# Decoder layer with product-key experts: 26 instead of 22 key sums computed as dense blocks, gate sums used straight from PSUM, table places and chunk spacing changed

## The chip, the cores and the metric

The kernel runs on one core of one Trainium2 chip. The metric is device time in microseconds of one launch; lower is better. TensorE (PE) multiplies matrices into PSUM, VectorE (DVE), ScalarE (ACT) and GpSimd (POOL) do the rest, SyncE (SP) and GpSimd's queue start the DMA transfers, and 16 DMA engines carry them all.

## What is computed

One decoder layer for 256 tokens of width 1024: two kinds of self attention, a cross attention, and then the part that the change is about, a product-key expert layer:

```python
def peer(h, w_q, sub_keys, u, v):
    q = (hf @ w_q).reshape(T, PEER_HEADS, 2, PEER_KEY_DIM // 2)
    sc = jnp.einsum('thpc,pkc->thpk', q, sub_keys).astype(jnp.float32)
    v1, i1 = lax.top_k(sc, PEER_TOPK)                       # 16 of 128 keys, twice
    ...                                                     # 16 best of the 256 pairs
    gates = jax.nn.softmax(top, axis=-1)
    def token_block(args):
        xc, ec, gc = args
        a = jax.nn.gelu(jnp.einsum('cd,ced->ce', xc, u[ec]), approximate=False)
        return jnp.einsum('ce,ced->cd', gc * a, v[ec])
```

Each of 256 tokens picks 8 x 16 = 128 of 16384 experts. An expert has a row of `u` and a row of `v`, 1024 floats each. A final rmsnorm follows.

## The kernel before

**Gathered slots.** The 32768 (token, expert) pairs are worked off in 256 slots. A slot is one expert for each of 128 tokens: GpSimd starts an indirect DMA that fetches up to 128 rows of 8 KB (`u` and `v` side by side) into a buffer of a ring; DVE multiplies the `u` half with the token's row and sums (`dot`, L2266); ACT applies gelu, the gate, and writes the weight on a diagonal matrix (`weigh`, L1608, L1614, L1622); PE multiplies diagonal by `v` half and sums in PSUM (`use_pair`, L1211 and L1214). PE, ACT and the buffers go by groups of two slots: group i holds slots 2i and 2i+1. Slots 0 to 127 belong to the first 128 tokens, 128 to 255 to the others.

**Blocks.** Expert rows are sorted on the host by key sum, (first key - second key) mod 128. The first 106 key sums (`GATHERED_KEYS`) are gathered. The other 22 (`BLOCKS`) are blocks of 128 experts that are computed densely for all 256 tokens; rows of theirs in a slot are left out of the gather by its bounds check. A block needs a 512 KB table of `u`, an *up product* (8 matmuls of 128x256, `up_product`, L1261), gelu into `in_block_acts` (`take_up`, ACT), a multiplication with the token's gate, and a *down product* with a 512 KB table of `v` (4 matmuls of 128x512 for both halves of the tokens, `weigh_block`, L1294).

**Tables.** SP loads the 44 tables in order (L801) into `tables`, four places: two over `x`, two over buffers given up by the ring. Table j waits until table j-4 has been used.

**Gate sums.** How much gate a token gives to each expert of the blocks is found in 16 chunks of 16 tokens. For a chunk DVE builds a one-hot matrix (`onehot`, L2315) and, for every second chunk, a list of gates (`listed_gates`, L2330 and L2335); PE multiplies them (`token_gates`, 32 small matmuls, L1282) into a PSUM bank; ACT copies the bank to `gate_sums` (`take_gates`, L1693); DVE multiplies it onto the activations (`weigh_acts`, L2342). Before a chunk's `weigh_acts` DVE waits for that copy.

**The order** is written out by hand in tables that are keyed by slot (DVE) or by group (PE, ACT). Up products stand behind groups 36 to 58; chunk q starts at slot 118 + 4q, its `token_gates` stands behind group (start + 2) // 2, its `weigh_acts` at slot start + 7; down products stand behind groups 94 to 116, two (block, half) pairs in most. Each engine's queue is in order. The ring has 12 to 14 buffers at first; five are given up for activations, one-hots and tables between slots 67 and 104, which leaves 10; one joins at slot 134 and one at slot 194 (`JOINS`). Gather n is issued only when PE has used the slot that had its buffer.

Of the kernel before, what the change touches and what calls it, by code (L numbers as in the profile page):

```python
# [17 lines left out]
D = 1024  # L18
S = 256
# [51 lines left out]
QUERIES_FIRST = 3  # L71


BLOCKS = 22
GATHERED_KEYS = PEER_KEYS - BLOCKS
GATHERED = GATHERED_KEYS * PEER_KEYS
EXPERTS = PEER_KEYS * PEER_KEYS
# [43 lines left out]

TURN_BEHIND = {7: 0, 9: 1}
TAKE_TURN_BEHIND = {8: 0, 10: 1}
UP_FROM, UP_TO = 36, 60
UP_PARTS = 1
UP_BEHIND, TAKE_UP_BEHIND = {}, {}
for n in range(UP_PARTS * BLOCKS):
# [6 lines left out]
COUNT_AT = 90  # L134
ONEHOT_AT = {}
GATHER_GATES_BEHIND = {}
TAKE_GATES_BEHIND = {}
WEIGHTS_AT = {}
for q in range(TOKEN_CHUNKS):
    begun = 118 + 4 * q  # L140
    ONEHOT_AT[begun] = q
    GATHER_GATES_BEHIND[(begun + 2) // GROUP] = q
    TAKE_GATES_BEHIND[(begun + 2) // GROUP + 1] = q
    WEIGHTS_AT[begun + 7] = q
DOWN_FROM, DOWN_TO = 94, 117
# [24 lines left out]
RAW_LOADED = [name for name in PANELS if name not in LOADED_EARLY]  # L170
FIRST_BUFFERS = [0, 5, 8, 2, 3, 4, 9, 10, 11, 12]
PRODUCT_BUFFER = 13
JOINS = {22: 14, 24: 15, 58: 6, 67: 7, 79: 1, 134: 16, 194: 11}
JOINED_BEHIND = {134: f"up{BLOCKS // 2 - 1}", 194: f"token_gates{TOKEN_CHUNKS - 1}"}
GIVEN_FROM = {15: 67, 14: 70, 10: 86, 11: 102, 12: 104}
BACK = {JOINS[n]: n for n in JOINED_BEHIND}

# [62 lines left out]
def product_order():  # L240


    order = []

    def add(name, engine):
        order.append((name, engine))

    for c in range(4):
        add(f"turn_mix{c}", "both")
    for j in range(15):  # L250
        add(f"qkv{j}", "act")
        if j == 0:
            add("line", "dve")
            add("keys", "act")
    for r in range(SOFTMAXES):
        for s in self_slots(r):
            add(f"score{s}", "dve")
        if r in GATE_AFTER_SCORES:
            add(f"gate{GATE_AFTER_SCORES[r]}", "act")
    for r in range(SOFTMAXES + 1):  # L260
        if r < SOFTMAXES:
            for s in self_slots(r):
                add(f"probs_t{s}", ("act", "dve")[s % 2])
        if r in GATE_AFTER_TURN:
            add(f"gate{GATE_AFTER_TURN[r]}", "act")
        if r >= 1:
            add(f"self_o{r - 1}", "both")
    for c in range(4):
        add(f"turn_mem{c}", "both")
    for branch in "AB":  # L270
        for c in range(4):
            add(f"branch{branch}{c}", "dve")
    add("kv0", "act")
    add("kv1", "act")
    for j in range(4):
        add(f"out{j}", "dve")
    add("kv2", "act")
    for c in range(4):
        add(f"turn_cross{c}", "both")
    add("kv3", "act")  # L280
    for j in range(2):
        add(f"qcross{j}", "act")
    for h in range(CROSS_HEADS):
        add(f"cross_score{h}_0", "act")
    for i in range(2):
        add(f"cross_probs_t{i}_0", "act")
    for i in range(2):
        add(f"cross_o{i}_0", "both")

    def cross_output(t):  # L290
        for j in range(2):
            add(f"ocross{j}_{t}", "dve")

    def turned_rows(t):
        for half in range(2):
            add(f"turn{t}_{half}", "both")

    def query(h, t):
        add(f"qpeer{h}_{t}", "act")
# [12 lines left out]
    add("cross_o0_1", "act")
    add("cross_o1_1", "act")
    cross_output(1)
    query(1, 0)
    turned_rows(1)
    for kind in ("qpeer", "qturn", "key_score"):
        for h in range(2):
            add(f"{kind}{h}_1", "act")
    query(2, 0)  # L320
    query(2, 1)

    for i in range(GROUPS):
# [12 lines left out]
        if i in GATHER_GATES_BEHIND:
            add(f"token_gates{GATHER_GATES_BEHIND[i]}", "act")
    return order


# [33 lines left out]
def build(nc, x_in, mem_in, rel_bias, panels, keys_in, experts, up_in, gain_cols, gain_rows, ident_in,  # L374
          onehot_in, mask_in, iota_in, count_in, out):
    with ExitStack() as ctx:
# [145 lines left out]
        def slot(n):  # L522
# [17 lines left out]
        in_block_acts = given[:, 0:BLOCKS * S].rearrange("p (b t) -> p b t", b=BLOCKS)  # L540
        onehots = [given[:, at:at + PEER_KEYS * CHUNK // 2].bitcast(F16).rearrange("p (e t) -> p e t", e=PEER_KEYS)
                   for at in (8 * D, 9 * D)]
        gate_sums = given[:, BLOCKS * S:BLOCKS * S + SUMS * CHUNK * BLOCKS].rearrange("p (s b t) -> p s b t", s=SUMS, b=BLOCKS)
        tables = [x[:, 0, :], x[:, 1, :]] + [given[:, at:at + D] for at in (6 * D, 7 * D)]
        last_squares, gained = given[:, 5 * D:6 * D], given[:, 6 * D:6 * D + 512]

        by_lists = scores.rearrange("p (u c) -> p u c", u=UNITS)
# [134 lines left out]
        count_step = sem("count_step")  # L682
        onehot_step = sem("onehot_step")
        onehot_ready = sem("onehot_ready")
        blocks_gated = sem("blocks_gated")
        blocks_weighed = sem("blocks_weighed")
        crossed_out = sem("crossed_out")
        crossed_summed = sem("crossed_summed")
# [120 lines left out]
        def _(pe):  # L809
# [477 lines left out]
            def weigh_block(block, t):  # L1287

                if block == 0:
                    pe.wait_ge(blocks_gated, TOKEN_CHUNKS)  # L1290
                down = table(BLOCKS + block)
                for half in range(2):
                    cols = slice(half * 512, (half + 1) * 512)
# [72 lines left out]
        def _(act):  # L1366
# [316 lines left out]
                    took(nc.scalar.copy(rowsT[:, 4 * half:4 * half + 4, t * P:(t + 1) * P],  # L1683
                                        b.rearrange("p (k c) -> p k c", k=4)))

            def take_gates(q):

                b = take(f"token_gates{q}")
                if q == 0:
                    act.wait_ge(slot_free, LAST_IN[12] + 1)  # L1690
                if q >= SUMS:
                    act.wait_ge(blocks_gated, q - SUMS + 1)
                took(nc.scalar.activation(gate_sums[:, q % SUMS], b[:, 0:CHUNK * BLOCKS].rearrange(  # L1693
                    "p (b t) -> p b t", b=BLOCKS), ACT.Copy, scale=1.0 / GATE_SCALE))
# [21 lines left out]
            def take_up(j):  # L1716

                b = take(f"up{j}")
                if j % 4 == 0:
                    act.wait_ge(slot_free, LAST_IN[(14, 10, 12)[j // 4]] + 1)  # L1720
                took(nc.scalar.activation(in_block_acts[:, 2 * j:2 * j + 2, :].rearrange("p a b -> p (a b)"), b,
                                          ACT.Gelu))

# [9 lines left out]
            for i in range((UNITS - 1) * TOPK // GROUP):  # L1733
# [27 lines left out]
                    take_row_turn(TAKE_TURN_BEHIND[i])  # L1761
                if i in TAKE_UP_BEHIND:
                    take_up(TAKE_UP_BEHIND[i])
                if i in TAKE_GATES_BEHIND:
                    take_gates(TAKE_GATES_BEHIND[i])
                if i == PEER_HEADS * TOPK // GROUP:
                    for half in range(2):
                        take_crossed(0, half, PEER_HEADS * TOPK)
# [34 lines left out]
        def _(dve):  # L1803
# [533 lines left out]

            def weigh_acts(q):

                dve.wait_ge(taken["act"], taken_count(f"token_gates{q}"))  # L2340
                part_of_acts = in_block_acts[:, :, q * CHUNK:(q + 1) * CHUNK]
                nc.vector.tensor_tensor(part_of_acts, part_of_acts, gate_sums[:, q % SUMS], ALU.mult  # L2342
                                        ).then_inc(blocks_gated, 1)

            def last_weight_diag(s):

# [276 lines left out]
```

## Time and profile before

| | us |
|---|---|
| median of 3 runs (lowest, highest) | 916.57 (915.57, 924.42) |
| the profiled execution, its own time | 915.18 |
| its span, first to last instruction | 913.1 |
| PE, DVE, ACT, POOL busy in it | 821.2, 643.6, 419.8, 388.4 |

The span is 2.1 us shorter than the execution's own time. Attention and the first queries take the first 300 us; the gathers run from about 295 to 900. PE is busy 90% of the span, but in some stages it waits and in others it never does, so the rows below are read by stage. A busy DMA share of 1.00 means all 16 engines were busy all the time.

### The profile page before, as it was taken

The page shows a single profiled execution, that of the slowest core. Times are in us where ns is not written, and L with a number is a line of the kernel's source. Part 1 is how long each engine was busy: PE and PEld are TensorE (multiplying, and loading weights), DVE is VectorE, ACT ScalarE, POOL GpSimd, SP SyncE. Part 2 cuts the span into 40 slices and gives each one's busy share as a digit, 9 for nine tenths or more (in the row PEclk, how much of TensorE's full clock was granted, in tenths as well). Part 3 has the DMA queues.
Part 4 walks back from the last instruction along what each step waited for, and adds up shares of the span by engine and source line. Part 5 has one row for each costly group of instructions (what it writes and reads, how often), then busy time and mean ns, then how long its engine had stood idle before and what let it go on. Part 6 is the DMA issues. An engine that isn't in the chain of part 4 may idle for free.

```text
span 913.1 us, 15434 instructions
## 1 busy us (share of the span) xinstructions
PE 821.2 (90%) x5656; PEld 528.7 (58%) x5656; DVE 643.6 (70%) x1467; ACT 419.8 (46%) x1075; POOL 388.4 (43%) x307
## 2 busy tenths in 40 slices
PE   9999999999999778697699999989778869999975
PEld 8999998799987634354256666634334423333311
DVE  5444686465657897979998999968888754444565
ACT  6534556345556566445455446433344332222243
POOL 1000055122002577466664444557757744434470
PEclk9999999999999999898999999979999889999988
DMA  8898434156353999999999999999999999999993
GB/s 303 236 228 231 169 119 159 55 215 251 127 207 125 367 377 420 417 406 417 417 416 416 415 410 412 412 416 416 419 416 415 419 418 408 415 416 415 412 397 148
DMA packets 55602, 302.62 MB, mean 331 GB/s; under 512 B 11904, under 2 KB 15348, under 8 KB 22674
## 3 DMA queue, kind: packets, MB, share of 16 engines
q0 software_dynamic: 37152, 222.64, 59.7%
q1 hardware_dynamic: 15544, 76.13, 22.9%
q10 hardware_dynamic: 2832, 2.88, 2.3%
q8 instruction: 44, 0.72, 0.3%
q14 instruction: 30, 0.25, 0.1%
HBM read 345.90 MB, written 1.54 MB: 381 GB/s over the span
## 4 chain that ended last, share of the span: by engine, by line
PE 63%; DMA 14%; DVE 9%; ACT 6%; issue 6%; POOL 2%; POOLq 0%; SPq 0%; DVEq 0%; ACTq 0%
PE y L1211 15%; PE ps L1261 9%; DMA arena<-in_experts,arena 8%; PE y L1294 8%; PE ps L825 6%; PE ps L826 6%; PE ps L827 6%; DVE late_ring L2266 3%; PE ps L868 2%; DMA rowsT<-in_experts,arena 2%; DVE w_lo L1818 2%; DMA late_ring<-in_experts,arena 2%; DMA late_ring<-in_experts,expert 2%; ACT w_hi L1388 1%; ACT diag L1622 1%
## 5 line engine op out<-in xcount | busy, mean ns | idle before, releaser
L2474 POOL DMA_INDIRECT arena<-in_experts,arena x148 | 197.8, 1337 | 154.2 <-PE ps L1214 116.4
L2266 DVE CUSTOM_DVE_ANT_0 late_ring<-arena 128x1024 f32<-128x1024 f32 x158 | 192.2, 1222 | 83.4 <-DMA arena<-in_experts,arena 75.1
L1211 PE MATMUL y<-arena,diag 64*64 64x512 f32 x600 | 154.5, 637 | 43.1 <-ACT diag L1622 39.6
L1214 PE MATMUL ps<-arena,diag 64*64 64x512 f32 x616 | 157.8, 633 | 0.0
L1608 ACT ACTIVATE acts<-dots 128x2 f32<-128x2 f32 x125 | 25.3, 202 | 256.9 <-DVE dots L2266 234.9
L1818 DVE TENSOR_TENSOR w_lo<-raw,w_hi 128x2048 fp32r<-128x2048 f32 x36 | 84.9, 2360 | 70.2 <-ACT w_hi L1388 70.2
L2266 DVE CUSTOM_DVE_ANT_0 late_ring<-late_ring,arena 128x1024 f32<-128x1024 f32 x82 | 99.7, 1220 | 30.5 <-DMA late_ring<-in_experts,arena 23.3
L2474 POOL DMA_INDIRECT late_ring<-in_experts,arena x63 | 80.4, 1276 | 73.8 <-PE ps L1214 61.6
L1211 PEld LDWEIGHTS y<-arena,diag 64*64 64x64 f32 x600 | 37.5, 137 | 127.9 <-issue 69.7
L1211 PE MATMUL y<-late_ring,diag 64*64 64x512 f32 x328 | 82.5, 624 | 21.6 <-ACT diag L1622 19.8
L1388 ACT CAST w_hi<-raw 128x2048 fp32r<-128x2048 f32 x37 | 70.4, 1904 | 50.2 <-DMA raw<-in_panels 36.9
L1622 ACT ACTIVATE diag<-ident,acts 128x128 f32<-128x128 f32 x250 | 86.8, 394 | 4.8 <-PE ps L1214 0.8
L825 PE MATMUL ps<-h_hi,w_hi 128*128 128x256 f32 x304 | 86.9, 286 | 0.0
L826 PE MATMUL ps<-h_lo,w_hi 128*128 128x256 f32 x304 | 86.0, 283 | 0.0
L827 PE MATMUL ps<-h_hi,w_lo 128*128 128x256 f32 x304 | 86.0, 283 | 0.0
L2446 POOL TENSOR_SCALAR arena<-arena,row_inv 128x128 f32<-128x128 f32 (+3 forms) x24 | 25.7, 1084 | 119.6 <-DVE row_inv L1887 119.4
L1214 PE MATMUL ps<-late_ring,diag 64*64 64x512 f32 x280 | 70.0, 619 | 0.0
L825 PEld LDWEIGHTS ps<-h_hi,w_hi 128*128 128x128 f32 x304 | 58.3, 192 | 2.3 <-issue 2.0
L826 PEld LDWEIGHTS ps<-h_lo,w_hi 128*128 128x128 f32 x304 | 58.3, 192 | 0.0
L827 PEld LDWEIGHTS ps<-h_hi,w_lo 128*128 128x128 f32 x304 | 58.3, 192 | 0.0
L1211 PEld LDWEIGHTS y<-late_ring,diag 64*64 64x64 f32 x328 | 20.2, 136 | 64.4 <-issue 35.9
L1614 ACT ACTIVATE acts<-acts,arena 128x1 f32<-128x1 f32 x218 | 52.3, 287 | 4.4
(359 smaller groups left out, 1796.3 us busy)
## 6 DMA issues: line engine op xcount, KB each, us to landing
raw<-in_panels SPq DMA_DIRECT2D x40, 1024.0 KB, 4.9
arena<-in_panels SPq DMA_DIRECT2D x6, 1024.0 KB, 7.1
x<-in_up SPq DMA_DIRECT2D x12, 512.0 KB
late_ring<-in_experts SPq DMA_DIRECT2D x12, 512.0 KB
late_ring<-in_up SPq DMA_DIRECT2D x10, 512.0 KB
x<-in_experts SPq DMA_DIRECT2D x10, 512.0 KB
arena<-line_scratch ACTq DMA_DIRECT2D x8, 320.0 KB, 7.8
arena<-in_experts,arena POOLq DMA_INDIRECT x148
```

What stands on the lines that cost most here:

```text
L825: pe.matmul(dst, stationary[0], moving[0], start=first, stop=False)
L826: pe.matmul(dst, stationary[0], moving[1], start=False, stop=False)
L827: return pe.matmul(dst, stationary[1], moving[0], start=False, stop=last)
L1211: straight = pe.matmul(y[rows, t, cols], diag[rows, a % DIAGS, rows], slot(a)[rows, down], start=False, stop=False, skip_group_check=True)
L1214: across = pe.matmul(ps[to, half, :], diag[rows, b % DIAGS, rows], slot(b)[rows, down], start=first, stop=False, skip_group_check=True)
L1261: mm = pe.matmul(b[:, block % 2 * S:(block % 2 + 1) * S], up[:, k * P:(k + 1) * P], rowsT[:, k, :], start=(k == 0), stop=(k == CHUNKS - 1))
L1294: mm = pe.matmul(y[:, t, cols], in_block_acts[:, block, t * P:(t + 1) * P], down[:, cols], start=False, stop=False, skip_group_check=True)
L1388: nc.scalar.copy(split_parts(n)[0], raw_panel(n)).then_inc(w_hi_ready, 1)
L1622: i = nc.scalar.activation(diag[:, s % DIAGS, :], ident[:], ACT.Copy, scale=acts[:, s:s + 1])
L1818: nc.vector.tensor_tensor(low, raw_panel(n), high.bitcast(F32), ALU.subtract).then_inc(w_lo_ready, 1)
L2266: i = nc.vector.tensor_tensor_reduce(row if n < len(FIRST_BUFFERS) else products[s % GROUP], row, h_rows[:, u // PEER_HEADS, :], 1.0, 0.0, ...
L2474: nc.gpsimd.indirect_dma_start(out=slot(n), out_offset=None, in_=experts, in_offset=bass.IndirectOffsetOnAxis(ap=expert_rows(u)[:, s:s + 1 ...
```

## The change

- `BLOCKS` goes from 22 to 26, so 102 key sums are gathered. Four more up products, down products and pairs of tables; all chunk operands over blocks grow from 22 to 26 columns.
- The tables have three places instead of four: the activations now reach into the buffer that held two of them.
- `take_gates` on ACT and `gate_sums` are gone. `weigh_acts` reads the PSUM bank itself, scales and multiplies in one DVE operation, and waits for `token_gates` on PE.
- Up products stand behind groups 34 to 59. Chunks start every three slots, at 118 + 3q, and `weigh_acts` stands six slots after the start instead of seven. Down products stand behind groups 86 to 116, one or two pairs each. The ring gets its buffer back at slot 180 instead of 194.

```diff
-BLOCKS = 22
+BLOCKS = 26
...
-UP_FROM, UP_TO = 36, 60
+UP_FROM, UP_TO = 34, 61
...
 for q in range(TOKEN_CHUNKS):
-    begun = 118 + 4 * q
+    begun = 118 + 3 * q
     ONEHOT_AT[begun] = q
     GATHER_GATES_BEHIND[(begun + 2) // GROUP] = q
-    TAKE_GATES_BEHIND[(begun + 2) // GROUP + 1] = q
-    WEIGHTS_AT[begun + 7] = q
-DOWN_FROM, DOWN_TO = 94, 117
+    WEIGHTS_AT[begun + 6] = q
+DOWN_FROM, DOWN_TO = 86, 117
...
-JOINS = {22: 14, 24: 15, 58: 6, 67: 7, 79: 1, 134: 16, 194: 11}
+JOINS = {22: 14, 24: 15, 58: 6, 67: 7, 79: 1, 134: 16, 180: 11}
...
-            add(f"token_gates{GATHER_GATES_BEHIND[i]}", "act")
+            add(f"token_gates{GATHER_GATES_BEHIND[i]}", "dve")
...
-        tables = [x[:, 0, :], x[:, 1, :]] + [given[:, at:at + D] for at in (6 * D, 7 * D)]
+        tables = [x[:, 0, :], x[:, 1, :]] + [given[:, at:at + D] for at in (BLOCKS * S,)]
...
-            def take_gates(q):
-
-                b = take(f"token_gates{q}")
-                if q == 0:
-                    act.wait_ge(slot_free, LAST_IN[12] + 1)
-                if q >= SUMS:
-                    act.wait_ge(blocks_gated, q - SUMS + 1)
-                took(nc.scalar.activation(gate_sums[:, q % SUMS], b[:, 0:CHUNK * BLOCKS].rearrange(
-                    "p (b t) -> p b t", b=BLOCKS), ACT.Copy, scale=1.0 / GATE_SCALE))
...
             def weigh_acts(q):
 
-                dve.wait_ge(taken["act"], taken_count(f"token_gates{q}"))
+                if q == 0:
+                    dve.wait_ge(taken["act"], taken_count(f"up{BLOCKS // 2 - 1}"))
+                b = take(f"token_gates{q}")
                 part_of_acts = in_block_acts[:, :, q * CHUNK:(q + 1) * CHUNK]
-                nc.vector.tensor_tensor(part_of_acts, part_of_acts, gate_sums[:, q % SUMS], ALU.mult
-                                        ).then_inc(blocks_gated, 1)
+                took(nc.vector.scalar_tensor_tensor(part_of_acts, b[:, 0:CHUNK * BLOCKS].rearrange(
+                    "p (b t) -> p b t", b=BLOCKS), 1.0 / GATE_SCALE, part_of_acts, ALU.mult, ALU.mult))
```

PE around the start of the up products, before. L868 is the last query product, L1211 and L1214 use a group of slots (four rows a group), L1180 is a key score, L1261 an up product:

```order
2144 L868 MATMUL ps<-rowsT,arena 128x256 x8
2145 L1211 MATMUL y<-late_ring,diag 64x512 x2
2146 L1214 MATMUL ps<-late_ring,diag 64x512 x2
2147 L1211 MATMUL y<-late_ring,diag 64x512 x2
2148 L1214 MATMUL ps<-late_ring,diag 64x512 x2
2149 L1211 MATMUL y<-arena,diag 64x512 x2
2150 L1214 MATMUL ps<-arena,diag 64x512 x2
2151 L1211 MATMUL y<-arena,diag 64x512 x2
2152 L1214 MATMUL ps<-arena,diag 64x512 x2
2153 L1180 MATMUL ps<-keysT,qpT 128x128 x4
```

The same place after; its lines are five lower, so L1256 is the up product:

```order
2144 L863 MATMUL ps<-rowsT,arena 128x256 x8
2145 L1206 MATMUL y<-late_ring,diag 64x512 x2
2146 L1209 MATMUL ps<-late_ring,diag 64x512 x2
2147 L1206 MATMUL y<-late_ring,diag 64x512 x2
2148 L1209 MATMUL ps<-late_ring,diag 64x512 x2
2149 L1256 MATMUL ps<-rowsT,x 128x256 x8
2150 L1206 MATMUL y<-arena,diag 64x512 x2
2151 L1209 MATMUL ps<-arena,diag 64x512 x2
2152 L1206 MATMUL y<-arena,diag 64x512 x2
2153 L1209 MATMUL ps<-arena,diag 64x512 x2
2154 L1175 MATMUL ps<-keysT,qpT 128x128 x4
2155 L1256 MATMUL ps<-rowsT,x 128x256 x8
```

Groups 34 and 35 have up products behind them now, where they stood back to back. The second place is DVE in the middle of the chunks, before (L2266 is a dot, whose second row reads out its sum):

```order
1004 L2342 TENSOR_TENSOR late_ring<-late_ring 128x22x16
1005 L2266 ISA late_ring,dots<-arena 128x1024
1006 L2266 ISA dots 128x1
1007 L2315 TENSOR_TENSOR late_ring<-counts,column_of 128x2048
1008 L2266 ISA late_ring,dots<-late_ring,arena 128x1024
1009 L2266 ISA dots 128x1
1010 L2266 ISA late_ring,dots<-arena 128x1024
1011 L2266 ISA dots 128x1
1012 L2266 ISA late_ring,dots<-arena 128x1024
1013 L2266 ISA dots 128x1
1014 L2342 TENSOR_TENSOR late_ring<-late_ring 128x22x16
```

And after, where L2249 is a dot, L2327 `weigh_acts`, L2298 `onehot`, L2313 and L2318 `listed_gates`:

```order
1014 L2327 SCALAR_TENSOR_TENSOR late_ring<-ps,late_ring 128x26x16
1015 L2298 TENSOR_TENSOR late_ring<-counts,column_of 128x2048
1016 L2249 ISA late_ring,dots<-arena 128x1024
1017 L2249 ISA dots 128x1
1018 L2249 ISA late_ring,dots<-arena 128x1024
1019 L2249 ISA dots 128x1
1020 L2249 ISA late_ring,dots<-arena 128x1024
1021 L2249 ISA dots 128x1
1022 L2327 SCALAR_TENSOR_TENSOR late_ring<-ps,late_ring 128x26x16
1023 L2313 TENSOR_TENSOR raw<-raw,row_of 128x832
1024 L2318 TENSOR_TENSOR gates_even<-raw,gate_piece 128x1664
1025 L2298 TENSOR_TENSOR late_ring<-counts,column_of 128x2048
```

There were four dots between two `weigh_acts`; there are three. Between a chunk's `onehot` and its `weigh_acts` there are six dots instead of seven.

## Rows read from the trace of the kernel before

**Rows 1.** Busy time by stretch; columns PE, PEld, DVE, ACT, POOL, then PEclk, DMA share, GB/s.

```profile
300.00:340.00 40.00, 29.78 (x239) 18.77 (x237) 36.93 (x123) 23.47 (x67) 24.17 (x18) 1.00 0.95 374
346.00:473.00 127.00, 102.17 (x668) 52.08 (x657) 112.76 (x355) 66.89 (x209) 75.70 (x59) 0.93 1.02 416
473.00:597.00 124.00, 124.00 (x730) 77.26 (x722) 113.53 (x361) 62.61 (x192) 60.59 (x45) 1.00 1.02 413
597.00:706.00 109.00, 87.58 (x838) 44.30 (x834) 90.15 (x145) 42.16 (x146) 73.77 (x53) 0.92 1.02 417
706.00:745.00 39.00, 28.12 (x241) 11.60 (x241) 26.38 (x43) 13.23 (x48) 24.50 (x20) 0.85 1.02 418
745.00:867.00 122.00, 122.00 (x532) 43.23 (x528) 57.00 (x93) 31.77 (x116) 53.53 (x45) 0.99 1.01 414
867.00:896.00 29.00, 19.65 (x129) 5.18 (x132) 17.54 (x31) 13.29 (x39) 18.49 (x14) 0.84 0.99 398
```

**Rows 2.** DMA by queue: q0 the gathers, q1 SP's transfers; packets, MB, share.

```profile
q0 software_dynamic: 37152, 222.64, 59.7%
q1 hardware_dynamic: 15544, 76.13, 22.9%
```

**Rows 3.** The chain of work, up products: start us, us, what.

```profile
469.70 1.85 issue
...
473.51 3.65 PE ps L1261 x16
...
479.04 3.65 PE ps L1261 x16
...
597.21 0.65 PE y L1211 x2
```

**Rows 4.** The chain of work, down products.

```profile
751.53 3.63 PE y L1294 x8
...
757.04 3.63 PE y L1294 x8
```

**Rows 5.** DVE's groups from 600 to 745: busy us, mean ns, idle before.

```profile
L2266 DVE CUSTOM_DVE_ANT_0 late_ring<-arena 128x1024 f32<-128x1024 f32 x50 | 60.8, 1225 | 20.8 <-DMA arena<-in_experts,arena 16.6 <-issue 3.9
L2315 DVE TENSOR_TENSOR late_ring<-counts,column_of 128x2048 f16<-128x2048 f16 x14 | 17.1, 1219 | 0.0
...
L2342 DVE TENSOR_TENSOR late_ring<-late_ring 128x352 f32<-128x352 f32 x16 | 8.3, 521 | 1.3 <-ACT late_ring L1693 1.3
...
L2330 DVE TENSOR_TENSOR raw<-raw,row_of 128x704 f16<-128x704 f16 x7 | 3.6, 520 | 0.0
L2335 DVE TENSOR_TENSOR raw<-raw,gate_piece 128x1408 f16<-128x1408 f16 x4 | 3.6, 893 | 0.1
```

**Rows 6.** A DVE operation of the new kind, from PSUM, 128x512.

```profile
L2386 DVE SCALAR_TENSOR_TENSOR x<-y,rstd,raw 128x512 f32<-128x512 f32 x2 | 1.4, 746 | 0.0
```

**Rows 7.** Timeline inside a chunk: start us, us, engine, what, idle before.

```profile
644.96 1.22 DVE L2266 CUSTOM_DVE_ANT_0 late_ring<-arena 128x1024 f32<-128x1024 f32 x1
...
646.11 1.23 DVE L2266 CUSTOM_DVE_ANT_0 late_ring<-rowsT,arena 128x1024 f32<-128x1024 f32 x1
...
648.93 0.65 PE L1211 MATMUL y<-arena,diag 64*64 64x512 f32 x2 [0.41 <-ACT diag L1622]
...
650.81 2.22 PE L1282 MATMUL ps<-raw,late_ring 128*128 128x22 f16 x32
```

**Rows 8.** The chain of work: gathers from issue to landing, and a group at the lower clock.

```profile
642.57 14.02 DMA late_ring<-in_experts,arena
...
715.27 1.12 PE y L1211 x2
716.40 0.84 PE y L1211 x2
```

**Rows 9.** SP's timeline: a table is issued.

```profile
477.19 0.33 SPq L801 DMA_DIRECT2D x<-in_up  x1
```

**Rows 10.** DMA by queue, 480.2 to 484.4, behind that issue.

```profile
q1 hardware_dynamic: 143, 0.52, 31.1%
```

More of the change, by code:

```diff
@@ L82 @@
 PIECES = 2
-SUMS = 1
 TO_WHOLE = 1.5 * 2 ** 23
@@ L136 @@
 GATHER_GATES_BEHIND = {}
-TAKE_GATES_BEHIND = {}
 WEIGHTS_AT = {}
 for q in range(TOKEN_CHUNKS):
-    begun = 118 + 4 * q
+    begun = 118 + 3 * q
     ONEHOT_AT[begun] = q
     GATHER_GATES_BEHIND[(begun + 2) // GROUP] = q
-    TAKE_GATES_BEHIND[(begun + 2) // GROUP + 1] = q
-    WEIGHTS_AT[begun + 7] = q
-DOWN_FROM, DOWN_TO = 94, 117
+    WEIGHTS_AT[begun + 6] = q
+DOWN_FROM, DOWN_TO = 86, 117
 DOWN_BEHIND = {}
@@ L172 @@
 PRODUCT_BUFFER = 13
-JOINS = {22: 14, 24: 15, 58: 6, 67: 7, 79: 1, 134: 16, 194: 11}
-JOINED_BEHIND = {134: f"up{BLOCKS // 2 - 1}", 194: f"token_gates{TOKEN_CHUNKS - 1}"}
+JOINS = {22: 14, 24: 15, 58: 6, 67: 7, 79: 1, 134: 16, 180: 11}
+JOINED_BEHIND = {134: f"up{BLOCKS // 2 - 1}", 180: f"token_gates{TOKEN_CHUNKS - 1}"}
 GIVEN_FROM = {15: 67, 14: 70, 10: 86, 11: 102, 12: 104}
@@ L542, in build @@
                    for at in (8 * D, 9 * D)]
-        gate_sums = given[:, BLOCKS * S:BLOCKS * S + SUMS * CHUNK * BLOCKS].rearrange("p (s b t) -> p s b t", s=SUMS, b=BLOCKS)
-        tables = [x[:, 0, :], x[:, 1, :]] + [given[:, at:at + D] for at in (6 * D, 7 * D)]
+        tables = [x[:, 0, :], x[:, 1, :]] + [given[:, at:at + D] for at in (BLOCKS * S,)]
         last_squares, gained = given[:, 5 * D:6 * D], given[:, 6 * D:6 * D + 512]
@@ L684, in build @@
         onehot_ready = sem("onehot_ready")
-        blocks_gated = sem("blocks_gated")
         blocks_weighed = sem("blocks_weighed")
@@ L1289, in weigh_block @@
                 if block == 0:
-                    pe.wait_ge(blocks_gated, TOKEN_CHUNKS)
+                    pe.wait_ge(taken["dve"], taken_count(f"token_gates{TOKEN_CHUNKS - 1}"))
                 down = table(BLOCKS + block)
@@ L1719, in take_up @@
                 if j % 4 == 0:
-                    act.wait_ge(slot_free, LAST_IN[(14, 10, 12)[j // 4]] + 1)
+                    act.wait_ge(slot_free, LAST_IN[(14, 10, 12, 15)[j // 4]] + 1)
                 took(nc.scalar.activation(in_block_acts[:, 2 * j:2 * j + 2, :].rearrange("p a b -> p (a b)"), b,
@@ L1763, in _ @@
                     take_up(TAKE_UP_BEHIND[i])
-                if i in TAKE_GATES_BEHIND:
-                    take_gates(TAKE_GATES_BEHIND[i])
                 if i == PEER_HEADS * TOPK // GROUP:
```

## The prediction

> **What bounds the kernel now.** I read the windows by stage first, since PE's 821.2 of 913.1 us is an average over stages with different limits. From 346 to 867 the DMA engines are busy all the time at 413 to 418 GB/s [rows 1]: the reader is to see that this column hardly moves while PE's does. PE is busy throughout in two stages, 473 to 597 (up products) and 745 to 867 (down products), and waits in the others. So both are near their limits. What separates them is the chain of waits: in the two product stages it runs along PE, one block and one group of slots each 5.53 us (up: 473.51 to 479.04) and 5.51 us (down: 751.53 to 757.04) [rows 3, 4]; elsewhere it steps over to gathers of 14.0 us from issue to landing [rows 8]. A gather carries 222.64 / 256 = 0.870 MB [rows 2], which is 2.09 us at 417 GB/s; 14.0 us are then 6.7 gathers in flight. Behind 867 PE has little left and the end hangs on the last 17 slots landing.
>
> **Bytes.** Gathers fall by 4 of 106 key sums: 222.64 x 4/106 = 8.40 MB less; 8 more tables of 0.524 MB are 4.19 MB more. Net 4.21 MB, at 415 GB/s 10.1 us. Some 20 slots run before the engines are full (374 GB/s at share 0.95 [rows 1]), where PE, DVE and the issuing set the pace; I give them no saving: 20 x 0.033 MB = 0.66 MB, 1.6 us. If the DMA engines stayed as full as they are, the end would come 8.5 us earlier.
>
> **Up products.** Four more cost 4 x 3.65 = 14.6 us of PE [rows 3], in a stage where PE has no gap. Two things give back. The groups before it come some 4.5 us earlier through fewer bytes (about 70 slots x 0.033 MB, less the first 20, and one table less ahead: 1.65 + 0.52 MB would be 5.2 us; I take 4.5), and between groups 35 and 36 PE stood still for 1.85 us [rows 3], about 2 with its surroundings. So group 60, which starts at 597.2 [rows 3], starts at 597.2 + 14.6 - 4.5 - 2 = 605.3. The transfers need less than that: a group now asks for 2 x 0.837 + 0.524 = 2.20 MB in 5.53 us, 397 GB/s, where 413 were moved [rows 1]. PE binds alone here, and over 26 blocks the engines lose 26 x 5.53 x (1 - 397/413) = 5.6 us. Part is only borrowed: the number in flight can fall first. How low it may fall before engines idle the trace doesn't show; from 6.7 down to about 5 is 1.7 slots, 3.4 us, and I take 3 us lost (between 0 and 5.6).
>
> **Chunks.** DVE's work for six slots (two chunks, one list) now: six dots at 1.15 us (back to back, start to start [rows 7]) 6.9; two one-hots 2 x 1.22 = 2.44; list 0.52 x 832/704 + 0.89 x 1664/1408 = 1.67; two `weigh_acts`. The new operation has no row of its own: the old one is 0.52 us for 352 columns, one of the same kind from PSUM 0.75 for 512 [rows 5, 6]; I take 0.62 for 416, nearer to the second in kind (0.58 to 0.75). Sum 12.25 us, 2.04 a slot, against 0.837/0.417 = 2.01 for the transfer. Before, eight slots with the same two chunks were 9.2 + 2.44 + 1.41 + 1.04 = 14.1 us, 1.76 a slot against 2.09, which is why DVE waits for gathers there [rows 5]. **The cover is gone.** The 16 ACT copies that are removed lay on an engine that was busy 42 of 109 us [rows 1], and DVE waited 1.3 us for them in all [rows 5]: nothing by themselves. The wait of `weigh_acts` moves to PE. From the end of the second dot of a group PE starts it after 1.67 us (646.11 + 1.15 = 647.26 to 648.93), the group takes 1.88 (to 650.81) and the 32 gate products 2.2 [rows 7]: 5.8 us. For an even chunk DVE fills this with `weigh_acts`, one-hot and three dots, 0.62 + 1.22 + 3.45 = 5.3, so it waits 0.5 to 0.65; for an odd one the list lies between as well and there is no wait. Behind that wait stand DVE's dots, and behind these ACT and PE. So 12.9 us for six slots, 2.15 a slot. Groups 60 to 86 (52 slots) become about 111 us, where they were 706 - 597 = 109. Group 86 starts at 605.3 + 111 = 716. The transfers of this stage, 52 x 0.837 + about 0.8 MB of tables, would take 106 us: 4 to 5 us more lost.
>
> **Down products.** They start behind group 86: 31 groups x 1.88 + 52 x 1.815 = 152.7 us on PE, if nothing waits, against 31 x 2 x 0.837 + 23 x 0.524 = 64 MB, 154 us, for the transfers. These balance; the last down product ends at about 869, where it ended at 867 [rows 1]. PE gets the 10 us back that it was late, because it now has work in 706 to 745, where it was busy 28 of 39 us.
>
> **The end.** By bytes: 913.1 - 8.5 + 3 + 4 = 911.6. By the chain: 869 instead of 867, but with some two slots more landed by then (2 x 1.93), so 913.1 + 2 - 3.9 = 911.2. I take a span of 911.2; with the 2.1 us around it 913.3, 1.9 below the profiled execution's 915.2. The median of the runs was 1.4 above that execution, so 914.7.
>
> **One rule weighed.** The trace has gathers only in a crowd, so it shows 14.0 us and not how few would do [rows 8]. The Trainium skill, "DMA: Bandwidth & Descriptors", section "Bandwidth", gives 6.15 us of engine time for a single 1 MB transfer. By that three or so in flight would keep the engines full, the up products would lose nothing, and the end would be another 3 us earlier, an estimate from that page. The row at 374 GB/s and share 0.95 speaks against taking it whole. The sum doesn't use it.
>
> **Rivals.**
> 1. *The transfers stay full.* The queue in flight absorbs both late stages and bytes alone decide: 8.5 us less, 908 span, about 908 to 909 as median. For: the share is 1.02 in every stage, even with 10 buffers. Against: 397 GB/s asked for by a stage in which PE has no gap is arithmetic, not a guess.
> 2. *Slower: the wait of `weigh_acts` on PE.* The even chunks' handshake has nothing to spare. A group at the lower TensorE clock takes 1.12 + 3 x 0.84 = 3.64 us instead of 1.88 [rows 8], and the granted clock averaged 0.92 in this stage, after PE had waited for diagonals. If most even chunks meet that, DVE waits 2.3 instead of 0.6 us, eight times: 13 us later at group 86. The rest of the program cannot make it good, as the down stage is full on both sides. With 0 to 5 us more from fewer gathers in flight: 924 to 931. It decides from about 0.5 us of delay per chunk. The Trainium skill, "TensorE: Matmul & The Clock Gate", section "HAM oscillation", tells of a kernel whose clock falls at every wait for DMA; by that each such group would be slow here too. The trace shows it for some groups, and PE will have fewer gaps than before.
> 3. *Three table places stall PE.* A table issued at 477.19 has all its 0.52 MB moved by 484.4, 7.2 us [rows 9, 10]. With three places it has two periods and a group, 2 x 5.53 + 1.87 = 12.9 us. Only if a table took as long as a gather (14.0) would PE wait, 1.1 us at each of some 48 tables, 50 us at most; I count 930 to 945.
>
> **How the numbers follow.** Forecast (908 to 921 around 914.7) 0.68; rival 1 (904 to 909) 0.12; rival 2 (922 to 931) 0.16; rival 3 0.04. One per cent, 9.2 us, is about what a measurement of this kernel can tell from no change. Faster by over that (below 907.4) takes most of rival 1 and a little of the forecast's edge: 0.12. Slower by over that (above 925.7) takes two thirds of rival 2 and rival 3: 0.15. The range leaves out the lower half of rival 1, the upper part of rival 2 and rival 3: 907 to 926.
>
> **What the profile after would show.** Gathers 214 MB, SP's queue 80 MB. PE without a gap from about 461 to 605, with 5.53 us between up products; GB/s in that stage about 400 instead of 413. Six slots in the chunks take 12.9 us, DVE is busy over 90% of it, and a new row has `weigh_acts` of 0.62 us waiting for L1277, 4 to 8 us in all. Down products end near 869. Rival 1 shows 413 or more in all stages; rival 2 shows waits over 12 us on L1277 and group 86 behind 722; rival 3 shows up products that wait for a table. I am wrong if DVE reaches the chunks so far ahead that it never binds, or if the engines idle already with five in flight.

## The result and the profile after

The kernel after takes 927.35 us (median of 4, 925.6 to 929.44) beside 916.07 before (4, 915.08 to 924.42): ratio 1.0116, interval 1.0089 to 1.0142, 11 us slower. The profiled execution took 929.44 us, 2.1 over the median. Its head and the page's rows on its queues and on two kinds of DMA (count, KB where given, median us from issue to landing):

```profile
span 927.6 us, 15608 instructions
...
q0 software_dynamic: 37152, 214.20, 58.0%
q1 hardware_dynamic: 16696, 80.32, 23.6%
...
arena<-in_experts,arena POOLq DMA_INDIRECT x146, 12.1
...
x<-in_up SPq DMA_DIRECT2D x18, 512.0 KB, 8.2
```

The bytes fell as the change says: 4.25 MB less than in [rows 2]. The same view by stage as [rows 1] (PE, PEld, DVE, ACT, POOL, PEclk, DMA share, GB/s), of after; its stages are: before the up products, up products, chunks, down products, the end:

```profile
346.00:468.00 122.00, 103.01 (x656) 51.25 (x656) 109.42 (x345) 69.46 (x212) 77.46 (x57) 0.92 1.01 413
468.00:611.00 143.00, 142.75 (x826) 90.91 (x826) 122.30 (x384) 64.96 (x203) 67.53 (x50) 1.00 0.98 380
611.00:722.00 111.00, 97.60 (x944) 52.71 (x946) 94.06 (x150) 37.29 (x133) 72.14 (x50) 0.91 0.98 381
723.00:881.00 158.00, 152.31 (x692) 52.27 (x692) 76.21 (x125) 42.70 (x155) 81.99 (x65) 1.00 1.02 416
881.00:910.60 29.60, 18.19 (x133) 4.45 (x132) 18.38 (x33) 14.08 (x42) 16.55 (x13) 0.94 1.00 411
```

Read the last column. Before, it stood at 413 to 418 up to 867. Now 254 us of the middle run at 380, first with PE busy without a gap, then with DVE waiting for PE. The engines' share shows almost nothing of it, 0.98 instead of 1.02. At 413 and 417 GB/s the same bytes would have taken 143 x (1 - 380/413) = 11.4 us and 111 x (1 - 381/417) = 9.6 us less.

The chain of work of after, where it turns from up products to chunks, inside the chunks, and in the down stage (start us, us, what):

```profile
468.25 3.72 PE ps L1256 x16
...
602.11 3.65 PE ps L1256 x16
607.64 3.65 PE ps L1256 x16
613.16 2.17 PE ps L1277 x32
...
676.12 0.83 PE y L1206 x2
676.98 0.83 PE y L1206 x2
679.80 2.17 PE ps L1277 x32
684.05 1.22 DVE late_ring L2298
```

The up products are on the chain one behind another, still 5.53 us apart as in [rows 3], 26 of them now. Behind them the chain goes PE (gate sums), DVE, PE, DVE. DVE's row for the new operation, 611 to 722 (busy us, mean ns, idle before), and then some of it in the timeline, with what DVE waited for:

```profile
L2327 DVE SCALAR_TENSOR_TENSOR late_ring<-ps,late_ring 128x416 f32<-128x416 f32 x16 | 9.4, 589 | 17.6 <-PE ps L1277 17.6
```

```profile
615.43 0.59 DVE L2327 SCALAR_TENSOR_TENSOR late_ring<-ps,late_ring 128x416 f32<-128x416 f32 x1 [7.58 <-PE ps L1277]
...
642.45 0.59 DVE L2327 SCALAR_TENSOR_TENSOR late_ring<-ps,late_ring 128x416 f32<-128x416 f32 x1 [0.63 <-PE ps L1277]
...
654.95 0.59 DVE L2327 SCALAR_TENSOR_TENSOR late_ring<-ps,late_ring 128x416 f32<-128x416 f32 x1 [0.63 <-PE ps L1277]
...
668.48 0.59 DVE L2327 SCALAR_TENSOR_TENSOR late_ring<-ps,late_ring 128x416 f32<-128x416 f32 x1 [1.74 <-PE ps L1277]
...
681.99 0.59 DVE L2327 SCALAR_TENSOR_TENSOR late_ring<-ps,late_ring 128x416 f32<-128x416 f32 x1 [1.72 <-PE ps L1277]
```

The first of the eight waits is PE's backlog: DVE is at chunk 0 at 607.9, PE still in its up products until 611.3. From there to 718 DVE waits for PE at these eight places and for no gather: it sets the pace of the chunks. Of the other seven (all at even chunks), two are 0.63 us and their six slots take 12.5 us; five are 1.7 to 1.8 us, and their six slots take 13.5. In front of the long ones PE's group runs at 0.83 us a pair of matmuls, as in the chain at 676.12, so at the lower of TensorE's two clocks (granted clock of the stage 0.91); just before it PE had stood 1.8 to 2.0 us for a diagonal, each time. In front of the two short ones PE had stood 0.3 to 0.5 us and its groups run at full speed.

The up stage in pieces, of after, and the piece of before that lies like the fourth:

```profile
478.00:500.00 22.00, 22.00 (x129) 13.79 (x128) 20.67 (x69) 9.75 (x31) 9.75 (x8) 1.00 1.00 400
500.00:520.00 20.00, 20.00 (x120) 12.03 (x119) 14.58 (x49) 9.85 (x31) 8.15 (x7) 1.00 0.97 357
520.00:540.00 20.00, 20.00 (x119) 13.01 (x121) 15.33 (x54) 12.67 (x37) 8.35 (x7) 1.00 1.01 406
540.00:558.00 18.00, 18.00 (x111) 10.76 (x102) 17.62 (x65) 5.79 (x23) 7.59 (x5) 1.00 0.87 307
558.00:611.00 53.00, 53.00 (x304) 34.01 (x303) 44.31 (x116) 24.43 (x74) 26.95 (x20) 1.00 1.00 394
```

```profile
540.00:558.00 18.00, 18.00 (x112) 10.76 (x108) 17.62 (x58) 8.77 (x27) 7.62 (x7) 1.00 1.01 409
```

So 380 is no steady rate. It is near 400 with two dips, to 357 and to 307.

### The profile page after: what moved, and what is told of

It is laid out like the page before. It is cut to its first block, busy times and chain, and to the rows that moved or that the text cites. A ratio compares the mean times of both kernels' runs of the same rounds, so it can differ in the third digit from the quotient of the medians.

```text
span 927.6 us, 15608 instructions
## 1 busy us (share of the span) xinstructions
PE 851.8 (92%) x5752; PEld 547.1 (59%) x5752; DVE 644.1 (69%) x1467; ACT 413.7 (45%) x1061; POOL 394.8 (43%) x307
## 4 chain that ended last, share of the span: by engine, by line
PE 62%; DMA 13%; DVE 12%; ACT 7%; issue 4%; POOL 1%; DVEq 0%; POOLq 0%; SPq 0%; ACTq 0%
PE y L1206 16%; DMA arena<-in_experts,arena 12%; PE ps L1256 10%; PE ps L820 6%; PE ps L822 6%; PE ps L821 6%; PE y L1289 5%; DVE late_ring L2249 4%; PE ps L1277 2%; ACT diag L1617 2%; PE ps L863 2%; DVE w_lo L1801 2%; ACT w_hi L1383 1%; PE ps L979 1%; DVE late_ring L2298 1%
## 5 line engine op out<-in xcount | busy, mean ns | idle before, releaser
L2459 POOL DMA_INDIRECT arena<-in_experts,arena x146 | 202.0, 1384 | 131.6 <-PE ps L1209 97.7
L2249 DVE CUSTOM_DVE_ANT_0 late_ring<-arena 128x1024 f32<-128x1024 f32 x158 | 191.1, 1221 | 69.7 <-DMA arena<-in_experts,arena 66.4
L1209 PE MATMUL ps<-arena,diag 64*64 64x512 f32 x736 | 191.7, 645 | 0.0
L1206 PE MATMUL y<-arena,diag 64*64 64x512 f32 x472 | 126.2, 661 | 23.6 <-ACT diag L1617 23.6
L1206 PE MATMUL y<-late_ring,diag 64*64 64x512 f32 x416 | 108.1, 642 | 21.1 <-ACT diag L1617 20.7
L2459 POOL DMA_INDIRECT late_ring<-in_experts,arena x65 | 83.5, 1285 | 89.2 <-PE ps L1209 72.4
L2249 DVE CUSTOM_DVE_ANT_0 late_ring<-late_ring,arena 128x1024 f32<-128x1024 f32 x82 | 99.5, 1218 | 27.1 <-DMA late_ring<-in_experts,arena 24.5
L1206 PEld LDWEIGHTS y<-arena,diag 64*64 64x64 f32 x472 | 30.9, 142 | 89.5 <-issue 50.4
L1206 PEld LDWEIGHTS y<-late_ring,diag 64*64 64x64 f32 x416 | 26.6, 140 | 81.1 <-issue 45.6
L1256 PE MATMUL ps<-rowsT,x 128*128 128x256 f32 x288 | 66.9, 385 | 1.3 <-ACT qpT L1641 1.3
L1256 PEld LDWEIGHTS ps<-rowsT,x 128*128 128x128 f32 x288 | 53.2, 190 | 21.7 <-issue 12.2
L1289 PE MATMUL y<-x,late_ring 128*128 128x512 f32 x136 | 64.4, 608 | 0.0
## 6 DMA issues: line engine op xcount, KB each, us to landing
arena<-in_experts,arena POOLq DMA_INDIRECT x146, 12.1
```

Of the source, the lines that this page charges most:

```text
L1206: straight = pe.matmul(y[rows, t, cols], diag[rows, a % DIAGS, rows], slot(a)[rows, down], start=False, stop=False, skip_group_check=True)
L1209: across = pe.matmul(ps[to, half, :], diag[rows, b % DIAGS, rows], slot(b)[rows, down], start=first, stop=False, skip_group_check=True)
L1256: mm = pe.matmul(b[:, block % 2 * S:(block % 2 + 1) * S], up[:, k * P:(k + 1) * P], rowsT[:, k, :], start=(k == 0), stop=(k == CHUNKS - 1))
L1289: mm = pe.matmul(y[:, t, cols], in_block_acts[:, block, t * P:(t + 1) * P], down[:, cols], start=False, stop=False, skip_group_check=True)
L2249: i = nc.vector.tensor_tensor_reduce(row if n < len(FIRST_BUFFERS) else products[s % GROUP], row, h_rows[:, u // PEER_HEADS, :], 1.0, 0.0, ...
L2459: nc.gpsimd.indirect_dma_start(out=slot(n), out_offset=None, in_=experts, in_offset=bass.IndirectOffsetOnAxis(ap=expert_rows(u)[:, s:s + 1 ...
```

## The experiments

Ratios are to the kernel before, timed on the same chip in the same job (median 915.2 to 916.2), with 95% intervals. Where a gain over the kernel after is given in us, it is the difference of two medians from different jobs; by the ratios it comes out up to 0.7 us smaller or larger. The first four were chosen to part the blocks, their PE time and their bytes from the rest.

**The blocks alone** (an edit of before; its chunks, down products and ACT copies are as they were):

```diff
-BLOCKS = 22
+BLOCKS = 26
-        tables = [x[:, 0, :], x[:, 1, :]] + [given[:, at:at + D] for at in (6 * D, 7 * D)]
+        tables = [x[:, 0, :], x[:, 1, :]] + [given[:, at:at + D] for at in (7 * D,)]
-                    act.wait_ge(slot_free, LAST_IN[(14, 10, 12)[j // 4]] + 1)
+                    act.wait_ge(slot_free, LAST_IN[(14, 10, 12, 15)[j // 4]] + 1)
```

> The kernel before with 26 blocks and nothing else of the change (three table places, because the activations cover the fourth; up products behind the old groups, chunks every four slots with the copy on ScalarE, down products behind groups 94 to 116). Theory A (four more products in a stage where PE has no gap slow it, and starve the transfers): up products end some 14 us later than before, the chunks go at the transfers' pace, down products end near 885, 926 to 932 us in all. Theory B (the three-slot chunks and DVE's wait on PE are what costs): chunks are as before here, so the time is at or below that of before, 908 to 917.

932.02 us, 1.0174 (1.0153 to 1.0196). The four blocks cost 16 us, more than the whole change. The windows of its up stage, of chunks and what follows up to the down products, and of the down products:

```profile
477.00:615.00 138.00, 138.00 (x793) 89.07 (x786) 116.89 (x365) 62.39 (x193) 61.36 (x47) 1.00 0.97 374
615.00:752.00 137.00, 111.92 (x1077) 55.69 (x1075) 113.59 (x182) 55.31 (x189) 97.36 (x70) 0.95 1.02 414
752.00:887.00 135.00, 135.00 (x564) 48.92 (x560) 61.15 (x100) 32.51 (x120) 58.48 (x48) 1.00 1.00 401
```

Most of the loss is in the up stage: 374 GB/s there, which is 138 x (1 - 374/413) = 13 us, and 414 behind it. A smaller part is in the down products, at 401 GB/s instead of 414: with the old start behind group 94 PE has no gap there either and sets the pace for 135 us, some 4 us of transfers. The rest of the change then gives 4.7 us of the 16 back. Its down stage, begun at group 86, runs at 416 GB/s.

**Everything but the blocks** (an edit of after):

```diff
-BLOCKS = 26
+BLOCKS = 22
-        tables = [x[:, 0, :], x[:, 1, :]] + [given[:, at:at + D] for at in (BLOCKS * S,)]
+        tables = [x[:, 0, :], x[:, 1, :]] + [given[:, at:at + D] for at in (6 * D,)]
```

> The changed kernel with 22 blocks again, all the rest of the change kept. Theory A: PE gets its 14.6 us back in the up products and as much in the down products, so it is near the kernel before, 912 to 919 us. Theory B: the chunk stage still has its waits of DVE on PE, so it stays 8 us or more above before, 924 to 928.

916.38 us, 0.9998 (0.9972 to 1.0023). Three places, sums from PSUM, chunks every three slots and down products from group 86 on make no difference with 22 blocks. Its three middle windows:

```profile
470.00:600.00 130.00, 128.50 (x767) 79.25 (x770) 120.19 (x381) 65.05 (x201) 64.22 (x50) 1.00 1.01 412
600.00:711.00 111.00, 95.95 (x946) 52.20 (x938) 94.16 (x154) 37.05 (x133) 72.45 (x52) 0.92 1.01 409
711.00:867.00 156.00, 140.98 (x660) 46.73 (x656) 75.08 (x123) 42.11 (x154) 74.55 (x63) 0.99 1.02 417
```

Against after, the up stage ends 11.7 us earlier (599.6, 611.3). The chunks take the same 111 us in both, and the down stage 156 against 158 us, although PE has 11 us less to do in it (141.0 against 152.3).

**The four more up products without their PE time** (an edit of after; one of the eight matmuls of each is left, the tables are loaded as before):

```diff
-                for k in range(part_of_it * chunks, (part_of_it + 1) * chunks):
+                chunks = CHUNKS if block < 22 else 1
+                for k in range(chunks):
...
-                                   start=(k == 0), stop=(k == CHUNKS - 1))
+                                   start=(k == 0), stop=(k == chunks - 1))
```

> The changed kernel, with the up products of the last four blocks cut to one of eight matmuls (the rest of those products is left out, the tables are still loaded): 12.8 us less PE work in the up stage alone. Theory A: 8 to 12 us faster than the changed kernel, 915 to 919 us. Theory B: at most 3 us faster, 924 or more.

922.12 us, 1.0058 (1.002 to 1.0095): 5.2 us back, which neither theory gave. PE has 12.8 us less of products (3.5 x 3.65), and the up stage ends 10.4 us earlier in the profile (600.9), of which 4.1 stood at slot 20 already (346.3 against 350.4), before any edit acts. The trace shows what kept the rest:

```profile
465.00:601.00 136.00, 131.13 (x770) 80.28 (x770) 118.43 (x378) 64.65 (x202) 65.21 (x48) 1.00 0.98 381
601.00:713.00 112.00, 97.62 (x942) 52.48 (x946) 97.95 (x157) 37.40 (x134) 74.13 (x53) 0.91 1.00 402
713.00:870.00 157.00, 152.46 (x696) 52.37 (x688) 76.28 (x124) 42.69 (x155) 79.31 (x65) 1.00 1.02 417
```

Only the last four blocks are short, so the first 22 still run PE at 5.53 us a group, and the rate of the stage stays at 381. At group 60 PE is then 3.9 us behind the start of slot 120's dot instead of 10.7: it has caught up with DVE, and waits for diagonals again (4.2 us). It could give back no more than PE was late, 6.8 us. The profiled execution (919.4) lies 2.7 below the median here, so the marks of its trace show more gain than the 5.2 us.

**Fewer bytes, same work on PE** (an edit of after: gathers skip rows of four more key sums, so 8.4 MB less is moved, with the tables as they are):

```diff
-bounds_check=GATHERED - 1,
+bounds_check=GATHERED - 4 * PEER_KEYS - 1,
```

> The changed kernel, with the rows of four more key sums left out of the gathers (their part of the result is left out): 8.4 MB less, 20 us of transfers at 416 GB/s, PE and DVE do the same. Theory A: nothing is gained in the up products and the chunks, which PE and DVE pace; only the down stage and the tail gain, 4 to 8 us, 919 to 923 us. If bytes still set the time throughout: about 20 us, 907.

923.04 us, 1.0065 (1.004 to 1.009). 8.4 MB are 20 us at 415 GB/s and bring 4.3.

```profile
468.00:611.00 143.00, 143.00 (x833) 90.88 (x826) 122.16 (x384) 64.92 (x203) 66.20 (x51) 1.00 0.96 367
611.00:721.00 110.00, 97.17 (x950) 51.98 (x948) 93.81 (x149) 37.30 (x133) 74.17 (x50) 0.92 0.98 366
721.00:877.00 156.00, 152.14 (x692) 52.33 (x688) 76.88 (x125) 42.70 (x155) 81.07 (x66) 1.00 1.02 416
```

This is the clearest reading of all: up stage 143 us as before it, chunks 110, and only GB/s fell. Where PE or the exchange of PE and DVE sets the pace, fewer bytes gain no time. The down stage, at 416 GB/s, did get 2 us shorter.

**The wait of `weigh_acts` alone**, two slots later:

```diff
-    WEIGHTS_AT[begun + 6] = q
+    WEIGHTS_AT[begun + 8] = q
```

> The changed kernel with the gates multiplied two slots later (start of the chunk + 8 instead of + 6), so that DVE finds the gate products done. If DVE's wait on PE lengthens the chunk stage and that is not made good later: the waits of 1.7 us at every second chunk go, the chunk stage is 6 to 9 us shorter, 920 to 923 us. If the down stage is bound by the transfers anyway and hides it: 926 to 928.

920.97 us, 1.0052 (1.0036 to 1.0068): 6.4 us back. DVE's waits in its chunks (waited for, us, times, longest):

```profile
DVE late_ring L2249 <- DMA arena<-in_experts,arena: 6.9, 9, 1.2
DVE late_ring L2298 <- PE ps L1277: 6.1, 3, 5.7
```

Of 17.6 us behind PE 6.1 are left, one of them PE's backlog of 5.7; DVE waits for gathers again, and its window shows the rate back at 409:

```profile
470.00:613.00 143.00, 142.31 (x824) 90.54 (x825) 123.47 (x386) 64.76 (x202) 66.86 (x51) 1.00 0.97 377
613.00:721.00 108.00, 96.97 (x949) 51.80 (x948) 93.90 (x149) 37.32 (x133) 73.45 (x54) 0.91 1.01 409
```

**The up products spread over more groups**, from group 31 (the load of `count_row`, which waits for the key scores, goes behind the eighth table on SP's queue instead of the third, so that it doesn't hold the earlier tables back):

```diff
-UP_FROM, UP_TO = 34, 61
+UP_FROM, UP_TO = 31, 61
-                if j == len(tables):
+                if j == 8:
```

> The changed kernel with the 26 up products from group 31 instead of 34, and the small transfer that waits for the last key score moved from table 3 to table 8 so that it holds no table back. PE has gaps of some 4 us before group 34 that three of the products can fill. If PE's work in a stage without a gap is the cost: up products end about 4 us earlier, 922 to 924 us. If something else sets the stage: no change, 926 to 928.

923.33 us, 1.0079 (1.0053 to 1.0105): 4 us back. Over the longer stretch the rate is 393 instead of 380:

```profile
450.00:606.00 156.00, 155.86 (x914) 98.94 (x914) 138.92 (x439) 76.65 (x236) 75.83 (x56) 1.00 0.99 393
```

**The four more blocks' down products at half their PE time** (an edit of after; one of the two halves of the output gets nothing from them):

```diff
-                for half in range(2):
+                for half in range(2 if block < 22 else 1):
```

> The changed kernel with the down products of the last four blocks cut to half (one of two matmuls; their part of the right half of the output is left out, tables still loaded): 7.3 us less PE work in the last groups of the down stage. If the down stage is bound by the transfers (416 GB/s in the changed kernel's trace), nothing is gained, 926 to 928. If PE paces it as my prediction had it: 5 to 7 us, 920 to 922.

928.48 us, 1.0121 (1.0087 to 1.0155): nothing gained. The down stage has 5.2 us less on PE and is as long; PE's waits in it grow from 5.6 to 9.8 us, behind diagonals that come behind dots:

```profile
722.00:879.00 157.00, 147.14 (x676) 49.61 (x672) 74.42 (x122) 41.59 (x152) 80.91 (x65) 0.99 1.02 416
```

```profile
PE y L1206 <- ACT diag L1617: 9.8, 8, 2.4
```

So that stage waits for transfers, not for PE.

**Three places for tables alone** (before, `(6 * D, 7 * D)` to `(7 * D,)`):

> The kernel before with three table places instead of four and nothing else. A table lands 7 to 8 us after its issue and has 12.9 us, so PE doesn't wait: within 2 us of before, 914 to 918. If the places matter, PE waits at most tables and it is 10 us or more slower.

916.61 us, 1.0006 (0.9991 to 1.002). From 477 to 867 PE waits for diagonals (28.1 us) and for no table. Rival 3 is out.

**Sums from PSUM alone** (before, with the parts of the diff on `weigh_acts`, `take_gates` and `token_gates`):

> The kernel before with nothing changed but the gate sums: VectorE multiplies them straight out of PSUM, ScalarE's copy is gone; 22 blocks, four places, chunks every four slots. The transfers are the limit there and VectorE has time: no change, 914 to 918 us. If the copy was on the path, 3 us or more faster.

916.85 us, 1.0003 (0.9986 to 1.0021). Nothing either, with the handshake: with four slots between chunks DVE waits 2.3 us for PE in all, and the chunks run at 417 GB/s.

**Both remedies together**, first with 26 blocks, then with 24:

```diff
-UP_FROM, UP_TO = 34, 61
+UP_FROM, UP_TO = 31, 61
-                if j == len(tables):
+                if j == 8:
-    WEIGHTS_AT[begun + 6] = q
+    WEIGHTS_AT[begun + 8] = q
```

> The changed kernel with both edits at once: up products from group 31, gates multiplied two slots later; 26 blocks. If the two losses are separate (4 us in the up stage, 6 in the chunks) they add: 916 to 919 us. If the down stage, bound by the transfers, takes one of them back: 920 to 922.

921.14 us, 1.005 (1.0027 to 1.0074). The gains of 4.0 and 6.4 us don't add, together they bring 6.2. Why is not shown.

> As the last kernel, with 24 blocks: 7.3 us less up work than with 26, and 2.1 MB (5 us) fewer bytes than with 22. If the count of blocks is a balance between PE's up stage and the bytes, this is the place to be: 911 to 915 us, below before. If the bytes saved are never worth anything, 916 or more.

918.28 us, 1.0023 (1.0008 to 1.0039). I had expected a version faster than before and was wrong. Two more blocks still cost 2 us.

**Both, and the last four up products short** (an edit of after, the three edits in one):

> 26 blocks with the spread up products and the later gate multiplication, and the up products of the last four blocks cut to one of eight matmuls (the rest left out, tables loaded): 12.8 us less PE work in the up stage. Both paces are lifted as far as they can be. If PE and DVE alone kept the 4.2 MB from being worth anything: the up stage ends near 597, the time is below that of before, 909 to 914 us. If the bytes were never worth 8 us, because the down stage moves as many as with 22 blocks: 915 to 918.

916.54 us, 1.0013 (0.9993 to 1.0034). With late waits and PE relieved of four blocks the chunks are back at 412 GB/s and the down stage at 416, but the up stage is at 386:

```profile
449.00:598.00 149.00, 143.59 (x849) 88.47 (x850) 132.16 (x425) 73.72 (x228) 75.43 (x54) 0.99 0.99 386
598.00:713.00 115.00, 97.49 (x948) 51.86 (x947) 101.19 (x163) 38.88 (x139) 77.79 (x55) 0.90 1.01 412
713.00:868.00 155.00, 152.48 (x692) 52.37 (x688) 76.03 (x123) 42.49 (x155) 77.97 (x63) 1.00 1.02 416
```

That is all the time of before with 4.2 MB less to move: the 8.5 us of bytes never appear. 386 GB/s instead of 415 over 149 us are 10 us of transfers, so the up stage still loses what the bytes save. No version beat the kernel before.

## Why the prediction was wrong

The span was forecast at 911.2 and came to 927.6, 16.4 us more. Marks counted out in the timelines, forecast and measured:

| mark, us (the first forecast is 605.3 less 26 x 5.53) | forecast | after | difference of the stretch |
|---|---|---|---|
| start of the up stage | 461.5 | 468.2 | +6.7 |
| its end, group 60 | 605.3 | 611.2 | -0.8 |
| group 86 | 716.3 | 721.0 | -1.2 |
| last down product ends | 869 | 881.0 | +7.3 |
| span | 911.2 | 927.6 | +4.4 |

**What held.** PE's terms did, nearly to the microsecond: 26 products at 5.53 us; 0.62 us for `weigh_acts` against 0.59; chunks of 111 us against 109.8; PE's waits for tables none. So the two stages that the change makes longer took the time that I gave them. The mistake is in what the transfers get to do in them.

**The step that failed: "I take 3 us lost (between 0 and 5.6)", and "4 to 5 us more lost".** The transfers lost 11.4 us in the up stage and 9.6 in the chunks, 21 instead of 7. By bytes alone that moves 911.6 to 925.6, 2.0 short of what came. The two terms are of the right kind, time in which the transfers get less to do than they can, and both are too small, for one reason: they count the gathers that PE *uses* in a stage. What the transfers get is the gathers that are *issued* and land in it. Counted in the timelines (a gather has landed when the packets of q0 have moved its bytes):

| start of | slots used | before: us, issued, landed | after: us, issued, landed |
|---|---|---|---|
| group 36 | 72 | 471.6, 84, 78.7 | 478.3, 85, 82.5 |
| group 60 | 120 | 597.2, 128, 125.5 | 611.2, 130, 127.0 |
| group 86 | 172 | 706.3, 181, 177.0 | 721.0, 180, 175.9 |
| (last down product ends) | 234 | 867.4, 245, 242.8 | 881.0, 245, 241.0 |

*In the up stage* I took "2 x 0.837 + 0.524 = 2.20 MB in 5.53 us, 397 GB/s". But between groups 36 and 60 three buffers leave the ring, behind slots 78, 93 and 94, and nothing is gathered into them: 48 slots are used and 45 gathers issued. Three of 0.837 MB in 132.9 us are 19 GB/s, so 378 were asked for, and 380 came. In time, 5.6 us of PE's pace and 2.5 MB / 413 GB/s = 6.1 us make 11.7, beside 11.4 measured. The dips lie behind the groups that free these buffers, 39 (from 494.9) and 46 and 47 (from 533.6). The kernel before gives away the same three and stays at 409 where after falls to 307 (all but the blocks: 389, from 540 to 560). It had more on the way: at 480 us both had landed 82.7 or 82.8 gathers, but before had issued 88, and after 85, because its PE, with up products behind groups 34 and 35 as well, had used four slots fewer. At group 60 PE was 7.4 us behind the start of slot 120's dot before (589.8, 597.2) and 10.7 after (600.5, 611.2). This is what I had called "borrowed" from the number in flight; after had already spent it on slots that had landed and waited for PE.

*In the chunks* I had 52 gathers in 111 us. DVE sets the pace there, and came into the stage ahead of PE: 49 dots and 48.9 landed gathers against 52 slots that PE used. The 3.1 gathers less are 6.2 us on top of my 4 to 5; 9.6 came. So what was landed and unused fell from 10.5 at group 36 to 7.0 at group 60 and 3.9 at group 86; before, it was 6.7, 5.5 and 5.0.

**"These balance", "PE gets the 10 us back".** It gets nothing back. The down stage from 723 moved 158 us x 416 GB/s = 65.7 MB, where I had 64 and two slots of advance: I had counted 62 gathers, as many as PE uses, and 65 landed. The three that the stages before had used up come back here, 2.5 MB or 6 us, most of the +7.3. It ran at the limit of the transfers (5 us of products taken off PE changed nothing), so every slot that was late at group 86 was late at the end. The two slots more landed that I took off the end (3.9 us) were never there, it was 1.8 fewer (241.0, 242.8); that is most of the +4.4. With 22 blocks and 11 us less on PE the stage is 156 us too.

**The bytes.** "If the DMA engines stayed as full as they are" was the condition, and I kept its 8.5 us while it failed in half the run. Where a stage is full of PE work, bytes saved are worth nothing (367 GB/s in the same 143 us). In the down stage slots 172 to 234 save 62 x 0.033 = 2.0 MB and four more tables bring 2.1: nothing there. What is left are the first 68 slots and the end.

**Rival 2** was right in kind and too large in size: waits of 1.7 us instead of 2.3, at five chunks. Its price was the 6.4 us that later waits give back; the 16 us of the blocks it cannot explain, as they come with the old handshake. What decided stood in no rival. The nearest was the last clause, "or if the engines idle already with five in flight", with no price, and it names another cause: the engines still moved 406 GB/s with about three gathers on the way (next paragraph). They moved less because less was issued.

**The rule weighed.** The three or so that I worked out from the Trainium skill, "DMA: Bandwidth & Descriptors", section "Bandwidth", were an estimate from its figure for one plain transfer. The trace does not speak against the number. From 520 to 540 a gather of after takes 8.7 us from issue to landing:

```profile
arena<-in_experts,arena POOLq DMA_INDIRECT x5, 8.7
```

With one used per 2.77 us that is 3.1 on the way, beside the tables, at 406 GB/s. In the down stage (740 to 870) the median is 22.8 us at 416 GB/s, about nine on the way. The 12.1 us in the profile above are the median over the whole run. What failed is the other half of my sentence, "the up products would lose nothing": with three on the way there is nothing to draw on when PE or a buffer that is given away holds the next one back.

**The start.** 4.6 of the first 6.7 us are there before any up product (DVE at slot 20: 345.8 before, 350.4 after). This varies from run to run with no relation to the edit: 348.5 and 349.4 in the two edits of before that cost nothing, 350.0 with 22 blocks, 346.3 in both_lifted. The profiled execution of before was the earliest of all at slot 20, so terms read from its absolute times may carry a luck of up to 3 us; its own time was 0.9 below the median of its runs. By medians the forecast missed by 12.7 us (914.7, 927.35).

**Open.** How the rate falls with the number in flight, apart from what is asked for: no run holds one fixed. Why the two remedies don't add. Why the start varies. That the three buffers and PE's lateness make the 380 of the up stage was counted, not tried by itself: no run keeps those buffers in the ring.

## What to carry to other kernels

In a kernel with two resources both near their limit, don't price an edit by the one whose load it lowers: list for each stage which of them sets the pace, and credit saved bytes only where the transfers do. Then count what the stage asks of the transfers: the transfers that are issued in it, not the buffers that are used in it. A buffer that leaves the ring asks for nothing, nor does a slot that had landed ahead and is merely used up; and such a reserve has to be fetched again later, in a stage that may be full. And split a change with parts that are meant to pay for each other: the blocks alone and all but the blocks told in two runs where the time went.

## What the runs showed of the hardware

- The busy share of the DMA engines hardly shows a loss of rate: 1.02 at 416 GB/s, 1.00 at 394 to 400, 0.98 at 380, 0.96 at 367, 0.87 at 307. A share of 0.98 is nearly a tenth below full here.
- A DVE product with one operand in PSUM takes no longer than from SBUF: 520 ns for 352 columns from PSUM (sums from PSUM alone) against 521 from SBUF [rows 5], and 589 for 416, 1.1 ns for a column more.
- About three gathers of 0.84 MB on the way, beside the tables, go with 406 GB/s, about nine with 416. Both counts are estimates, 8.7 and 22.8 us from issue to landing by the time between two gathers.
- A wait of PE for a diagonal of 1.8 to 2.0 us inside the chunks was followed by groups at 0.83 us a pair instead of 0.43 to 0.47, five times of five; the four waits of 0.3 to 0.5 us were not.
